# Opening of the first FFN: panel tiles one modulation step later in TensorE's order, with ScalarE's roundings, VectorE's low halves and two weight requests moved, and products of zeros between

## The reference, cut to what matters

```python
def modulation(cond, w_mod, b_mod):
    m = jax.nn.silu(cond) @ w_mod + b_mod
    return m.reshape(cond.shape[0], 1, N_MOD, D_MODEL)

def modulate(x, g, shift, scale):
    return rms_norm(x, g) * (1.0 + scale) + shift

def swiglu(h, w_in, w_out):
    g, u = jnp.split(h @ w_in, 2, axis=-1)
    return (jax.nn.silu(g) * u) @ w_out

x = x + m[2] * (0.5 * swiglu(modulate(x, norm_g[0], m[0], m[1]), w_in[0], w_out[0]))
```

## Time and profile before

| | us |
|---|---|
| median of 3 runs | 1666.42 |
| profiled execution, its own time | 1660.95 |
| its span, first to last instruction | 1659.0 |
| TensorE busy | 1565.6 (94%) |
| VectorE busy | 1115.1 (67%) |
| ScalarE busy | 648.0 (39%) |

### The profile page before, as it was taken

One profiled execution on the slowest core, in us unless ns is written; L12 is line 12 of the kernel. 1 busy time (PEld: TensorE's weight loads), 2 busy tenths in 40 slices (PEclk: granted clock), 3 DMA queues, 4 the chain that ended last, 5 costly groups with the idle time before them and its releaser, 6 DMA issues. The chain is left out here.

```text
span 1659.0 us, 21700 instructions
## 1 busy us (share of the span) xinstructions
PE 1565.6 (94%) x8783; PEld 1476.1 (89%) x8783; DVE 1115.1 (67%) x1827; ACT 648.0 (39%) x964; POOL 44.1 (3%) x47
## 2 busy tenths in 40 slices
PE   6999999899868999999999999989887999999999
PEld 4999999887548999999989999987765799999999
DVE  3788887778594787776668778764676757444332
ACT  4433323343473633333353333233336546333321
POOL 0000000000022000000000000000200000000000
PEclk8999999999998999999999999999899999999999
DMA  9565555533201455554535555642220013333233
GB/s 392 186 228 216 217 217 213 179 120 124 87 1 64 178 182 223 211 203 162 199 135 197 224 210 223 219 155 69 75 102 26 2 56 122 127 127 127 96 128 120
DMA packets 50563, 254.70 MB, mean 154 GB/s; under 512 B 6305, under 2 KB 8481, under 8 KB 34593
## 3 DMA queue, kind: packets, MB, share of 16 engines
q1 hardware_dynamic: 47888, 250.11, 41.6%
q10 hardware_dynamic: 2576, 3.22, 0.6%
HBM read 250.54 MB, written 2.77 MB: 153 GB/s over the span
## 5 line engine op out<-in xcount | busy, mean ns | idle before, releaser
L908 DVE TENSOR_TENSOR w_lo<-w_raw,w_hi 128x2048 fp32r<-128x2048 f32 (+2 forms) x186 | 375.8, 2020 | 237.7 <-ACT w_hi L546 236.6
L1510 PE MATMUL ps<-hx_hi,w_hi 128*128 128x384 f32 (+1 forms) x1472 | 501.0, 340 | 9.6 <-DVE hx_lo L990 9.2
L1511 PE MATMUL ps<-hx_lo,w_hi 128*128 128x384 f32 (+1 forms) x1472 | 499.2, 339 | 0.0
L1512 PE MATMUL ps<-hx_hi,w_lo 128*128 128x384 f32 (+1 forms) x1472 | 499.0, 339 | 0.0
L546 ACT ACTIVATE w_hi<-w_raw 128x2048 fp32r<-128x2048 f32 (+2 forms) x186 | 316.0, 1699 | 441.3 <-DMA w_raw<-in_w_out 223.5
L1510 PEld LDWEIGHTS ps<-hx_hi,w_hi 128*128 128x128 f32 x1472 | 279.0, 190 | 15.2 <-DVE hx_lo L990 14.0
L1511 PEld LDWEIGHTS ps<-hx_lo,w_hi 128*128 128x128 f32 x1472 | 278.5, 189 | 0.0
L1512 PEld LDWEIGHTS ps<-hx_hi,w_lo 128*128 128x128 f32 x1472 | 278.3, 189 | 0.0
L1512 PE MATMUL ps<-g_hi,w_lo 128*128 128x384 f32 x704 | 236.6, 336 | 0.0
L1510 PE MATMUL ps<-g_hi,w_hi 128*128 128x384 f32 x704 | 236.5, 336 | 0.0
L1511 PE MATMUL ps<-g_lo,w_hi 128*128 128x384 f32 x704 | 236.5, 336 | 0.0
(11 more groups left out here) (222 smaller groups left out, 1417.9 us busy)
## 6 DMA issues: line engine op xcount, KB each, us to landing
w_raw<-in_w_in SPq DMA_DIRECT2D x88, 1024.0 KB, 4.7
wm<-in_w_mod SPq DMA_DIRECT2D x128, 512.0 KB, 5.7
w_raw<-in_w_out SPq DMA_DIRECT2D x64, 704.0 KB, 4.1
w_raw<-in_w_qkv SPq DMA_DIRECT2D x12, 1024.0 KB, 4.8
wm_first<-in_w_mod_first SPq DMA_DIRECT2D x8, 1024.0 KB, 19.2
w_raw<-in_w_o SPq DMA_DIRECT2D x8, 1024.0 KB, 4.8
w_raw<-in_w_qup SPq DMA_DIRECT2D x8, 576.0 KB, 3.7
w_raw<-in_w_down SPq DMA_DIRECT2D x4, 1024.0 KB, 4.7
```

The lines of the kernel that those rows point to most:

```text
L908: nc.vector.tensor_tensor(w_lo[:, slot, 0:width], w_raw[:, slot, 0:width], w_hi[:, slot, 0:width].bitcast(F32), ALU.subtract).then_inc(w_l ...
L1510: nc.tensor.matmul(out, l_hi, r_hi, start=first, stop=False)
L1511: nc.tensor.matmul(out, l_hi, r_lo, start=False, stop=False)
L1512: return nc.tensor.matmul(out, l_lo, r_hi, start=False, stop=last)
```

## The change

- SyncE asks for panel 0 after wm_first 1 and for panel 1 after wm_first 2 (before: each one piece earlier).
- ScalarE does `high(0)` and `high(1)` in loop bodies 1 and 2, ahead of the normalization work, and `normed(k - 2)` in place of `normed(k - 1)`.
- VectorE does `low(0)` before `scaled(0)` in place of after it; `low(1)` keeps its place. It begins with a memset of `hn[:, 0, :]` to zero.
- TensorE does `both(k - 3)` ahead of `mod_rows(k)`, in place of `both(k - 2)` after it, and `mod_columns(k - 1)` after `mod_rows(k)`, in place of `mod_columns(k)`.
- TensorE multiplies the zeros of `hn` (128 x 128 by 128 x 384, fp32) into bank 4, whose contents are then overwritten: 5 products at the start, one before the sum of squares, one on either side of the broadcast, one after `mod_columns(1)`.

```diff
@@ sync
             for k in range(KD):
                 sp.dma_start(wm_first[:, k], d["w_mod_first"][k]).then_inc(wmf_loaded[k], 16)
-                if k < 2:
-                    load(k, "in", 0, k)
+                if k in (1, 2):
+                    load(k - 1, "in", 0, k - 1)
             load(2, "in", 0, 2)
@@ scalar, first_norm
+                    if k in (1, 2):
+                        high(k - 1)
                     if k == 1:
                         act.wait_ge(bc_ready, 1)
                         nc.scalar.activation(sqacc[:], ps[:, 6, 0:T], ACT.Copy).then_inc(rb_ready, 1)
-                    if k >= 1:
-                        normed(k - 1)
-                    if k < 2:
-                        high(k)
+                    if k >= 2:
+                        normed(k - 2)
+                normed(KD - 2)
                 normed(KD - 1)
                 high(2)
@@ vector
+            nc.vector.memset(hn[:, 0, :], 0.0).then_inc(zeros_ready, 1)
@@ vector, first_norm
                     one_plus_scale(0, 0, slice(k, k + 1))
+                    if k == 0:
+                        low(0)
                     scaled(0, k)
                     if k:
                         h_low(0, k - 1)
-                    if k < 2:
-                        low(k)
+                    if k == 1:
+                        low(1)
@@ tensor, ffn_in
+                    def idle(count):
+                        for _ in range(count):
+                            nc.tensor.matmul(ps[:, 4, 0:T], hn[:, 0, 0:P], hn[:, 0, :], start=True, stop=True)
+
+                    pe.wait_ge(zeros_ready, 1)
+                    idle(5)
                     pe.wait_ge(condT_ready, 1)
                     pe.wait_ge(pick_ready, 1)
                     for k in range(KD):
+                        if k >= 3:
+                            both(k - 3)
                         mod_rows(k)
                         if k == 0:
+                            idle(1)
                             sum_squares(0)
                         elif k == 1:
+                            idle(1)
                             broadcast(0)
-                        else:
-                            both(k - 2)
-                        mod_columns(k)
-                    both(KD - 2)
-                    both(KD - 1)
+                            idle(1)
+                        if k >= 1:
+                            mod_columns(k - 1)
+                        if k == 2:
+                            idle(1)
+                    mod_columns(KD - 1)
+                    for k in (KD - 3, KD - 2, KD - 1):
+                        both(k)
```

More of the change, by code:

```diff
@@ L258, in build_step @@
         pick_ready = sem("pick_ready")
+        zeros_ready = sem("zeros_ready")
         rows_ready = sem("rows_ready")
```

## The result

The changed kernel takes 1678.48 us in the median of 8 runs, against 1665.51 us for the kernel before in 8 runs beside it. The ratio is 1.0086, with a 95% interval of 1.0071 to 1.0102: 14.3 us slower (12 to 17); the two medians by themselves lie 13.0 us apart. The forecast was 13.8 us slower, at 1680.2 us. The profiled execution after has a span of 1673.3 us, 14.3 above the 1659.0 of before.

A forecast was written before the change was run, and what follows sets the result against it. TensorE was taken as the bound, busy 94% of the span, so the opening's delay moves the end. Terms 12.8 + 0.4 + 0.6 gave +13.8 us, 1680.2 us, range 1671 to 1687 us.

The forecast's parts named there:

- The end is moved by as much as panel 2: TensorE has no slack after the opening, so any shift of panel 2's first product, about 58.5 us, moves the end equally.
- The wait that nothing covers: Modulation steps: the block follows the columns at once and waits for VectorE and ScalarE, starting 2.7 us after the rows.
- Which clock: Four steps, rows 3 to rows 7: clock falls in the waits, 7.5 us a step, +12.8 us (bounds +5.8 and +16.6).
- Up to rows 3: Opening until rows 3 end: later weights and zeros put that at 31.3 against 30.91 us, +0.4 (bounds -2.1 and +1.4).
- The end: From rows 7's end to panel 2: columns 6 and 7 and three blocks, +0.6 us (bounds -0.9 and +4).
- The sum: The three terms 12.8, 0.4 and 0.6 give +13.8 us for the whole kernel, 1680.2 us.
- The clock holds in the steps: Rival: clock stays up in the modulation steps, +2.9 us, 1669.3 (+5.8 if only from rows 3 on); 14%.
- It never comes back: Rival: the clock stays at its lower level through the steps and the end, +22 us, 1688.4; 7%.
- Faster: Rival: the opening's clock gain outweighs the waits, needing steps of 5.0 us or less; -3.1 us, 1663.3, at 1.2 us waits; 5%.
- The page's rule: Opening: if activity releases the throttle, zeros bring the upper clock early, -2.1 us up to rows 3 instead of +0.4.

The follow-up runs named there:

- a2: The changed kernel with rows k moved ahead of block k-3 on TensorE; ratio to the kernel before 1.0008 (+1.3 us).
- a1: The changed kernel without its products of zeros; ratio to the kernel before 1.0095 (+15.8 us).
- a3: The changed kernel with three more products of zeros behind each step's columns from step 3, and five for one behind columns 1; ratio to the kernel before 1.0048.
- b5: The kernel before with VectorE's low half of block k-1 ahead of its wait for columns k, and panel 2's rounding and low half in bodies 5 and 6; ratio 0.9970.
- b1: The kernel before with the change's products of zeros alone; ratio to the kernel before 1.0006 (+1.0 us).
- b3: The kernel before with TensorE's new order alone (block k-3, rows k, columns k-1), no zeros; ratio to the kernel before 1.0062 (+10.3 us).
- b2: The kernel before with weight requests one piece later, panels 0 and 1 rounded ahead of normalization, first low half ahead of first scaled block; ratio 1.0019 (+3.2 us).
- c1: a2 plus VectorE's low half of block k-1 ahead of its wait for columns k, and panel 2's rounding and low half in body 5; ratio 0.9988.

## Why the prediction was right, point by point

- **The end is moved by as much as panel 2.** Panel 2's first product comes at 72.07 against 58.70, 13.4 us later (the prediction took the row at 58.53 for it, which is block 7's last); the mark is 13.9 and the span 14.3 us later. Right for this kernel. It does not hold for every pair of single profiles (below), and for a2 the timed runs don't follow the profile's opening either.
- **The wait that nothing covers.** Forecast 2.7 us from the rows to the block; it is 2.58. Four waits are 1.98 to 2.06 us. Block 5's was forecast at 2 us or more with the others and is 1.47, as the idle time is counted from both columns 6 and 7, which stand there in a row: a miss without weight.
- **Which clock.** "The block at the lower clock and the rows at the upper" holds for the two steps whose rows take 1.07 us (rows 6 and 7); rows 4 take 1.94 and rows 5 1.52. The four steps sum to 30.9 us (34.19 to 65.13), forecast 30.0. This nearness is in part luck: the blocks took 15.0 us where the forecast had 15.5, the waits 10.3 where it had 10.8, and the rows 5.6 where it had 3.7, as two of the four were not at the upper clock throughout. From rows 3's end, 31.61, to rows 7's, 62.56, it is 30.95 against 17.22: **+13.7** where the sum had +12.8.
- **Up to rows 3.** 31.61 against 30.91: **+0.7**, forecast +0.4. Here the prediction was right in part by luck: it had the second half of block 0 from 28.4 (it was 28.62), but rows 3 could have run at either clock. And it charged the zeros next to nothing there, where a1's profile, without them, has rows 3 end at 29.90, 1.7 us earlier.
- **The end.** 62.56 to 72.07 is 9.5 us against 10.6 (48.13 to 58.70): **-1.1**, forecast +0.6. This is the term that was mis-sized. The clock was up from 61 us on, TensorE finished its three blocks early (at 71.7) and waited 0.37 us for panel 2's low half. The bound of 9.4 us by ScalarE's and VectorE's chain was right, the choice of a value near TensorE's 11.2 was not: it took the clock to be low for the first block, as in the steps, while behind the wait of 1.47 us before block 5 the clock stayed at its upper level. In before it fell behind one of 1.51 us; why in one and not in the other stays open.
- **The sum.** 13.7 + 0.7 - 1.1 = 13.4 us (rounded once, at the end) in place of 13.8. The terms were off by +0.9, +0.3 and -1.7 us and cancel for the greater part; that the total is off by 0.4 only is luck, that the wait and the falling clock carry it is not.
- **Readings.** The rows cited for 416 GB/s have 413, and from the end of the columns to the scaled block it is 1.0 us and not 1.1. A block at the lower clock throughout took 4.14 us (34.19 to 38.33), where the prediction had 3.87. None of these moves the forecast by as much as its range.
- **The rivals.** "The clock holds in the steps" did not happen, but a3 made it so and found 6.4 us by the mark; the prediction had 5.8 if it holds from rows 3 on. "It never comes back" did not happen: the clock rose in each of the four steps. "Faster" needed a step of 5.0 us or less; no step comes near it, and a2 and b5 show what it would have taken, the covered wait.
- **The page's rule.** The Trainium skill, TensorE: Matmul & The Clock Gate (The HAM clock gate), says activity releases the throttle. a3 bears it out for products of zeros too: with them in the waits of the steps the granted clock is 1.00 from 20 us to panel 2, and without them it fell. The term that the prediction worked out by that page, -2.1 us up to the end of rows 3, did not come; it was +0.7. At the start the trace is less regular. With the same five products there, rows 0 take 1.07 us, the upper clock's time, in a2, a3 and b1, and 1.93 us in the changed kernel. That kernel gained nothing by them before block 0: behind its last product of zeros TensorE idles 3.18 us, and its products are spaced 0.32 us, the lower clock's, from 27 us on.

## What to carry to other kernels

When an item is moved in the list of an engine that works in order, write down for each wait which items lie between what starts the chain and what needs it: here the step count looked larger after the change, while the rows that had covered VectorE's chain and the block that had covered ScalarE's had moved out of it. Such cover is worth more than its length: by the marks, the new waits cost 6.4 us with the clock held up and another 7.5 by the clock that fell in them. Where a loop keeps a wait, first look whether the instruction waited for can stand ahead of its own engine's next wait; that, with panel 2's work moved into idle time, gave 5.0 us.

## What the runs showed of the hardware

The clock fell in steps of 6.96 us with one wait of 1.51 us (b3, granted clock 0.75), and held in steps of 4.22 us with one of 0.51 (a2, 1.00). A wait of 2 us was not followed by a fall each time: one step of a1, at 39.78, has 1.00 behind a wait of 2.04. With products of zeros in the 2 us waits it held in all steps (a3), though all their operands are zero.

One thing was not expected. Behind the mark all kernels run the same code, yet their profiles don't take the same time for it. From the mark to GpSimd's last power (L502, or L503 in kernels with a memset more) before has 1057.9 us (321.64 to 1379.51), and after, a2, b1, b2 and c1 have 1057.5 to 1058.6, but b5 has 1064.1, b3 1064.8, a1 1064.5 and a3 1070.3. Some 5 us of this lie between the mark and the third power already (229.3 us before, 234.8 in a1, 235.0 in b3, 234.4 in b5, 234.0 in a3). In the 25 us behind the mark, the rows of before, a1 and a3 differ so (busy times, granted clock, DMA share, GB/s):

```profile
321.64:346.64 25.00, 21.50 (x87) 17.42 (x88) 17.39 (x28) 13.88 (x21) 0.85 (x1) 0.86 0.29 106
332.85:357.85 25.00, 21.57 (x83) 17.43 (x84) 17.20 (x27) 12.92 (x20) 0.85 (x1) 0.80 0.27 101
327.99:352.99 25.00, 19.59 (x74) 15.82 (x75) 14.99 (x27) 12.07 (x18) 2.83 (x1) 0.76 0.25 92
```

The first is before's, with a granted clock of 0.86, the second a1's (0.80), the third a3's (0.76). GpSimd's power at the mark took 2.83 us in a3 and b5 and 0.85 or 0.86 in the others (at 1379.51 it takes 2.83 in before too). The longer power is not the whole cause, as a1 and b3 have it at 0.85 us and still take 6 to 7 us more behind the mark. What the cause is, and whether the lower clock is part of it or follows from it, was not tried. Between timed runs of one kernel the time goes with the mean granted clock: before's run of 1657.63 us has 0.982, that of 1668.34 has 0.974. So a single profile's end can hide or enlarge a shift in the opening: b5's mark is 5.7 us earlier and its last power 0.5 us later than before's, a3's are 6.4 and 18.8 us later, so that a mark right behind the change, and a ratio over several runs, are both needed.
